# Split exponentials without own waits, a chunk amid the value products, and rows of reciprocal norms by store and broadcast load

## The reference, cut to what matters

```
xn = rmsnorm(x, g_mix)                       # x: (4, 4096, 1024)
u  = xn @ w_in                               # 5120 columns: conv (3x512), q, k, v (512 each), gates (2x1024)
y_a = (b * causal_conv3(c * v_a)) @ w_a_out
s   = q k^T / 8 - slope_h * (qpos - kpos), causal       # 4 heads, two maps of 64 each, values of 128
o   = (softmax(s_1) - lam * softmax(s_2)) v
y_b = (rmsnorm(o) * 0.8) @ w_b_out
x   = x + (sigmoid(g_a) * y_a + sigmoid(g_b) * y_b) @ w_o
x   = x + relu(rmsnorm(x) @ w_mlp_in)^2 @ w_mlp_out
out = rmsnorm(x)
```

## Time and profile before

| what | value |
|---|---|
| median of 3 runs | 1164.12 us (1163.68 to 1166.56) |
| the profiled execution, its own time | 1163.79 us |
| its span on the slowest core (core 5) | 1162.2 us (cores 1160.2 to 1162.2) |
| PE busy | 1127.2 us, 97% |
| ACT, DVE, POOL busy | 47%, 40%, 7% |
| granted TensorE clock, mean of the cores | 0.995 to 0.998 |

### The profile page before, as it was taken

One profiled execution on the slowest core, in us unless ns is written; L12 is line 12 of the kernel. 1 busy time (PEld: TensorE's weight loads), 2 busy tenths in 40 slices (PEclk: granted clock), 3 DMA queues, 4 the chain that ended last, 5 costly groups with the idle time before them and its releaser, 6 DMA issues.

```text
span 1162.2 us, 20430 instructions; the slowest of 8 cores (1160.2 to 1162.2 us)
## 1 busy us (share of the span) xinstructions
PE 1127.2 (97%) x7162; PEld 563.0 (48%) x7162; DVE 466.9 (40%) x1051; ACT 550.3 (47%) x760; POOL 84.3 (7%) x136
## 2 busy tenths in 40 slices
PE   7999999999999999999999999999999999999997
PEld 3444555455455555555544444444444444444444
DVE  2476666644654632433435544222221322223212
ACT  2585786676666888878523223321231033003301
POOL 5212001001001001001100001000000000000000
PEclk8999999999999999999999999999999999999999
DMA  9877522332067059375296686911210140012001
GB/s 140 166 144 138 144 90 51 110 56 46 5 132 147 19 99 179 65 191 105 38 253 168 207 165 172 158 43 55 70 57 1 55 111 17 19 55 73 2 37 55
DMA packets 67491, 111.46 MB, mean 96 GB/s; under 512 B 37216, under 2 KB 40288, under 8 KB 66368
## 3 DMA queue, kind: packets, MB, share of 16 engines
q0 software_dynamic: 15056, 40.22, 22.5%
q1 hardware_dynamic: 52192, 69.68, 20.0%
q10 hardware_dynamic: 144, 0.26, 0.1%
HBM read 114.40 MB, written 29.36 MB: 124 GB/s over the span
## 4 chain that ended last, share of the span: by engine, by line
PE 92%; ACT 3%; DVE 2%; issue 2%; DMA 1%; POOL 0%; DVEq 0%; ACTq 0%; POOLq 0%
PE ps_all L441 92%; ACT big L715 2%; DMA big<-wv 1%; DVE big L780 0%; DVE big L594 0%; DVE big L604 0%; POOL big L484 0%; ACT big L852 0%; DVE big L772 0%; DVE big L863 0%; DVE big L574 0%; ACT big L592 0%; POOL big L446 0%; DVEq L152 0%; DVE big L571 0%
## 5 line engine op out<-in xcount | busy, mean ns | idle before, releaser
L441 PE MATMUL ps_all<-big 128*128 128x512 bf16 (+7 forms) x7162 | 1127.2, 323 | 28.9 <-ACT big L715 8.2
L441 PEld LDWEIGHTS ps_all<-big 128*128 128x128 bf16 (+2 forms) x7162 | 563.0, 98 | 592.9 <-issue 100.7
L715 ACT ACTIVATE big<-ps_all,big 128x1024 bf16<-128x1024 f32 (+3 forms) x384 | 338.3, 926 | 111.4 <-PE ps_all L441 104.4
L982 ACT ACTIVATE big<-ps_all 128x512 bf16<-128x512 f32 x128 | 76.5, 598 | 137.6 <-PE ps_all L441 137.4
L983 DVE TENSOR_TENSOR big<-big 128x512 bf16<-128x512 bf16 x128 | 54.5, 426 | 156.5 <-ACT big L982 156.0
L999 ACT ACTIVATE big<-big 128x1024 bf16<-128x1024 f32 x15 | 15.9, 1057 | 187.9 <-DVE big L994 187.9
L863 DVE SCALAR_TENSOR_TENSOR big<-big,ps_all 128x512 f32<-128x512 f32 x64 | 43.7, 687 | 106.3 <-PE ps_all L441 106.3
L994 DVE SCALAR_TENSOR_TENSOR big<-ps_all,big 128x512 f32<-128x512 f32 x30 | 22.5, 752 | 143.5 <-PE ps_all L441 143.5
L852 ACT ACTIVATE big<-ps_all,big 128x512 f32<-128x512 f32 x64 | 43.6, 686 | 67.7 <-PE ps_all L441 66.6
L898 ACT ACTIVATE big<-big 128x1024 bf16<-128x1024 f32 x16 | 16.9, 1057 | 47.0 <-DVE big L893 47.0
L724 DVE TENSOR_TENSOR big<-big 128x256 bf16<-128x256 bf16 x64 | 18.5, 289 | 46.7 <-ACT big L715 46.6
(11 more groups left out here) (90 smaller groups left out, 296.8 us busy)
## 6 DMA issues: line engine op xcount, KB each, us to landing
big<-xs SPq DMA_DIRECT2D x36, 512.0 KB, 6.8
big<-w POOLq DMA_DIRECT2D x32, 512.0 KB, 8.1
xm_sp<-big SPq DMA_DIRECT2D x16, 512.0 KB, 3.8
big<-xm_sp SPq DMA_DIRECT2D x16, 512.0 KB, 5.8
big<-xT POOLq DMA_DIRECT2D x31, 256.0 KB, 7.6
out<-big SPq DMA_DIRECT2D x15, 512.0 KB, 2.7
xn_sp<-big SPq DMA_DIRECT2D x4, 1024.0 KB, 6.6
big<-wg POOLq DMA_DIRECT2D x8, 512.0 KB, 5.9
```

Source lines behind the costliest of these rows:

```text
L441: S.op("pe", lambda e: e.matmul(out, lhsT, rhs, start=start, stop=stop, skip_group_check=skip), reads, writes)
L715: act(lambda e, a=a, b=b, c=c, s=s, PT=PT, scale=scale: e.activation(PT.ap[:, :, a:b], Sb[s][:, :, a:b], AF.Exp, bias=ccol(C_BTAB + c), sc ...
L982: act(lambda e: e.activation(r.ap, ps, AF.Relu), key, [r])
```

## The change

It has six parts. (1) `op` takes `part`, so the two exponentials of head 0 into one `PT`, and the three copies of the epilogue into `o_raw`, don't wait for each other. (2) `row` takes the place of `bcast` for blocks 1 to 3: a DMA on SP writes rs1 (128x4) to 512 words in HBM, and a second loads them to all 128 partitions of `R_b`. It stands as the last step of `stats`; the three `bcast` chunks leave `W`. (3) The DVE product that makes `ksc` is a step of its own (`scaled`), behind the one that makes rs1. (4) The statistics of block 1 are spread over 7 chunks, from the first pair on, and no longer over 4 from the fourth. (5) In the first pair of a head `pv(n, 0)` stands ahead of the chunk. `until` takes banks 0, 1, 2, 3, 7, starting so that, by the count of the chunks, the last has bank 7. (6) One copy of the halo goes from ACT to DVE.

```diff
+    def op(self, eng, fn, reads=(), writes=(), part=False):
+        return self._add(eng, fn, reads, writes, False, (), part)
...
         def last():
             rstd(rs1[blk], ss1[blk], 4)
-            if blk in ksc:
-                dve(lambda e: e.tensor_scalar_mul(ksc[blk].ap, rs1[blk].ap, 0.125), [rs1[blk]], [ksc[blk]])
+
+        def scaled():
+            dve(lambda e: e.tensor_scalar_mul(ksc[blk].ap, rs1[blk].ap, 0.125), [rs1[blk]], [ksc[blk]])
...
-        return [sq(0), sq(1), sq(2), sq(3), last]
+        return [sq(0), sq(1), sq(2), sq(3), last, scaled if blk in ksc else lambda: row(blk)]
...
+    def row(blk):
+        settle("norm%d" % (blk % 2))
+        S.dma("sp", lambda e: e.dma_start(out=rs_sp[blk].rearrange("(t p) -> p t", p=128), in_=rs1[blk].ap, allow_slow_non_contiguous=True),
+              [rs1[blk]], ["rssp%d" % blk])
+        ld(R_b[blk % 2].ap, rs_sp[blk:blk + 1].partition_broadcast(128), [R_b[blk % 2]], ["rssp%d" % blk])
...
-            act(lambda e: e.copy(hh.ap[:, lo:hi, :], v[:, :, 0, :]), ck, [hh])
+            dve(lambda e: e.tensor_copy(hh.ap[:, lo:hi, :], v[:, :, 0, :]), ck, [hh])
...
+            S.parts.discard(PT)
             for a, b, c in parts:
                 act(lambda e, a=a, b=b, c=c, s=s, PT=PT, scale=scale: e.activation(
                     PT.ap[:, :, a:b], Sb[s][:, :, a:b], AF.Exp, bias=ccol(C_BTAB + c), scale=scale),
-                    Sk[s] + [cst] + ([ksc[blk]] if blk in ksc else []), [PT])
+                    Sk[s] + [cst] + ([ksc[blk]] if blk in ksc else []), [PT], True)
...
-    W += [(0, f) for f in normed(0)] + spread(ks(5)[1:], [])
-    W += spread(vs(5), [halo_stat] + stats(1, 2) + wc_load(0))
+    W += [(0, f) for f in normed(0)]
+    W += spread(ks(5)[1:] + vs(5), stats(1, 2) + [halo_stat] + wc_load(0))
     W += spread(vs(1), xT_steps(2, 2))
-    W += [(1, bcast(1))]
...
-    def until(name, banks=range(8)):
+    def until(name, banks=range(8), turn=False):
         keep, oring[0] = oring[0], Ring(list(banks))
+        if turn:
+            oring[0].i = -sum(w for w, f in W[pos[0]:marks[name]]) % len(banks)
...
-                until(pairs[n + 1]["g"], (7, 0, 1, 2, 3))
+                until(pairs[n + 1]["g"], (0, 1, 2, 3, 7), True)
...
+        lead = p["first"] and n > 0
+        if lead:
+            pv(n, 0)
         if not p["last"]:
             work(2200 - (400 if diag else 0))
-        pv(n, 0)
+        if not lead:
+            pv(n, 0)
         pv(n, 1)
```

More of the change, by code:

```diff
@@ L103, in _add @@
         return ev
-    def op(self, eng, fn, reads=(), writes=()):
-        return self._add(eng, fn, reads, writes, False)
+    def op(self, eng, fn, reads=(), writes=(), part=False):
+        return self._add(eng, fn, reads, writes, False, (), part)
     def dma(self, eng, fn, reads=(), writes=(), extra=(), part=False):
@@ L263, in build_program @@
     xm_sp = dscr("xm_sp", [2048, D], F32)
+    rs_sp = dscr("rs_sp", [4, 512], F32)
     xb_sp = dscr("xb_sp", [2048, D], BF16)
@@ L431, in flush_masks, with act, dve @@
             late_masks.pop(0)()
[L434 to L438, removed]
+    def act(fn, reads, writes, part=False):
+        S.op("act", fn, reads, writes, part)
+    def dve(fn, reads, writes, part=False):
+        S.op("dve", fn, reads, writes, part)
     def mm(out, lhsT, rhs, start, stop, reads, writes, skip=False):
@@ L752, in out @@
             dve(lambda e: e.tensor_copy(o[:, m, 0:3, 0:129], bank(4 + m)[:, 0:390].rearrange(
-                "p (t e) -> p t e", t=3)[:, :, 0:129]), [pk(4 + m)], [o_raw])
+                "p (t e) -> p t e", t=3)[:, :, 0:129]), [pk(4 + m)], [o_raw], True)
+        S.parts.discard(o_raw)
         out(0)
         dve(lambda e: e.tensor_copy(o[:, :, 3, 0:129], bank(6)[:, 0:260].rearrange(
-            "p (m e) -> p m e", m=2)[:, :, 0:129]), [pk(6)], [o_raw])
+            "p (m e) -> p m e", m=2)[:, :, 0:129]), [pk(6)], [o_raw], True)
         out(1)
@@ L1195, in build_program @@
     W += [(0, f) for f in normed(1)]
-    W += spread(vs(2), []) + [(1, bcast(2))] + spread(ks(2)[:2], [])
+    W += spread(vs(2) + ks(2)[:2], [])
     c0 = [(1, f) for f in conv(0)]
@@ L1203, in build_program @@
     W += spread(conv(1)[:11], xT_steps(3, 1))
-    W += [(1, bcast(3))] + [(1, f) for f in conv(1)[11:]]
+    W += [(1, f) for f in conv(1)[11:]]
     W += spread(ks(3) + vs(3) + qs(3), xT_steps(7, 0) + stats(7, None))
```

## The result

The changed kernel takes 1183.91 us (median of 4 runs, 1182.22 to 1185.53) against 1164.05 us before: a ratio of 1.0166, 95% interval 1.0143 to 1.0189. It is some 20 us slower, where 11 us faster was forecast. Some runs have one half of the chip at a lower clock and are some per cent longer; the times and ratios here leave them out. The profiled execution took 1182.22 us, with a span of 1180.7 us on core 3.

What follows compares the result with a forecast made beforehand. PE was taken as the bound, busy 1127.2 of 1162.2 us, other engines mattering only where PE waits. Terms of 14.1 us less 3 given back left 11, so 1153 us from 1163.8; range 1147.5 to 1160.5.

Steps and rivals of the forecast that it cites:

- the two DMAs: Store and load on SP replacing `bcast`: some 7.5 us end to end, under some 20 us of cover, costed at 0.
- The rows come late: Rival: DVE stands at the first product reading `R_b`; decides from 31 us on, 1164 us or more; two slower rivals together 0.06.
- Halved exponentials: Head 0: up to 0.36 us off each of seven PE waits for exponentials; 2.2 us taken, 0.5 if ACT waits elsewhere.
- `ksc`: DVE's `ksc` product as a later step no longer waits for POOL, removing two PE waits: 2.4 us, half as low end.
- `pv(n, 0)` ahead: At heads' starts, value products between two chunks on bank 7 remove eight PE waits: 3.0 us, ends 0 and 4.1.
- Slower by the moved `pv`: Rival: 15 heads' starts each lose 1.0 us more, using up the gain: 1165 us or more; two slower rivals together 0.06.
- Own waits of the epilogue's copies: DVE's second copy at head ends starts 0.17 us late; PE needs copies later: taken as 0, perhaps up to 1 us.
- Banks: `until`: 0.85 us gained before the third group, about 0.9 us lost before the second; together 0, ends -1 and 0.9.
- Statistics, halo, copies: Block 1's statistics earlier 1.2 us (ends -0.5 and 2.4), halo's copy on DVE 0.3 us, epilogue's copies 0.
- The 3 us to be given back again: From the twelfth pair on chunks sit earlier: six new PE waits of about 0.5 us estimated, 3 us lost.
- The first term: Three `bcast` chunks leave PE and full chunks move into their slots: 5.0 us gained, ends 3.3 and 6.2.
- DVE waiting for a DMA ahead of a key's evacuation: Listed among the signs in the later profile that would show the forecast wrong; no size given.

Runs made afterwards that it cites:

- e4: Changed kernel with the three `bcast` back and the three single-word stores still issued but never loaded or read; 1164.83 us, ratio 1.0006.
- e9: Changed kernel with the three `bcast` back instead of the rows, and the `ksc` product back in the step that makes rs1; 1153.64 us.
- e5: Changed kernel with the three `bcast` back instead of the rows, and `pv(n, 0)` back behind the chunk; 1152.76 us.
- e11: Changed kernel with the three `bcast` back instead of the rows, and the first `until`'s banks counted with the halo's one; 1151.01 us.
- e10: Changed kernel storing rows in 16-byte pieces, POOL ordering them where `bcast` stood, the first `until`'s banks counted with the halo's; 1146.98 us.
- e2: Kernel before with only the rows by store and load in place of three `bcast`; 1210.4 us.
- e8: Changed kernel with `bcast` back and unread single-word stores, each word in 512 bytes of its own; 1154.15 us, one run.
- e3: Changed kernel with rows stored as 128 pieces of 16 bytes and `R_b` read with a 16-byte step; 1154.48 us, ratio 0.9913.
- e7: Changed kernel storing rows in 16-byte pieces, POOL ordering them at the end of `row`, the first `until`'s banks counted with the halo's; 1155.8 us.

## Why the prediction was wrong

**The step that failed** is that of the two DMAs, "That cover of some 20 us is why I cost it at 0". The cover was about right: the readers came 27 us (96.68 - 69.56) and 39 us after the issue, 4.3 and 16.2 us of it as waits, so 23 us each. What it had to cover was estimated at 7.5 us from rows that are no bound for it: `on_sp`'s small pieces and a load of 512 KB say nothing of 512 single words into one 2 KB. It was 26.9 us (15.89 + 11.00) and 39.2 us (31.61 + 7.57). The rival "The rows come late" named the place and the price of such a wait, but was held to be four times away; block 2's row went past its 31 us.

**What no case had** is that a slow store costs others: 14.2 us with no reader at all. Neither the sum nor a rival has a term for it. That all engines stop at once behind it is shown; by what is open. Of the third step's 11.9 us the unread store of `e4` accounts for 5.0. In after the waits of 7.9 us and the half clock behind them make nearly all of it, with no wait for a row; why the stand is longer than in `e4` stays open.

**The terms beside the rows** added up to 14.1 - 5.0 = 9.1 us, less 3 given back, 6. They gave some 14.
- Halved exponentials: 2.2, measured 7.0. The 0.18 us were right, the number of places was not. I counted only PE's waits over 0.15 us, seven of them, from the earlier trace rows. But in head 0 of the later groups nearly every pair with an own wait lasts longer by it, with waits of PE mostly too short for that list. What could be counted before is an upper end: 32 of head 0's 40 pairs have two own waits, and 64 of 0.18 us make 11.5 us; 7.0 is six tenths of that.
- `ksc`: 2.4, measured 3.0. In `e9` DVE waits for POOL 2.6 us again, as in the earlier trace rows.
- `pv(n, 0)` ahead: 3.0, measured 2.1, within its ends. In `e5` PE's short waits for L771 at heads' starts are back, 1.7 us in five. The rival *Slower by the moved `pv`* is refuted by it.
- Own waits of the epilogue's copies: held at 0, not tried alone. In the kernel before, DVE's second copy starts 0.73 us after the first, in after 0.47 us, as these lines of the two timelines show (see also the earlier trace rows; it is so in 12 and 14 of the 16 heads):

```profile
375.81 0.56 DVE L752 COPY big<-ps_all 128x387 f32<-128x387 f32 x1
376.54 0.43 DVE L755 COPY big<-ps_all 128x258 f32<-128x258 f32 x1 [0.17 <-PE ps_all L441]
```

```profile
64.75 0.56 DVE L761 COPY big<-ps_all 128x387 f32<-128x387 f32 x1
65.22 0.42 DVE L765 COPY big<-ps_all 128x258 f32<-128x258 f32 x1
```

Here an own wait costs DVE 0.26 us. The Trainium skill, in VectorE: DVE Perf Modes, section The DRAIN you can't avoid, says that the semaphore costs nothing extra; for these copies the trace does not agree. What it is worth to the kernel's time no run shows.

- Banks: the wait ahead of the second group came as counted, and none stands at the third. But its price was wrong: `e11` removes the 0.95 us and gains nothing.
- Statistics, halo, copies: 14.0 - 7.0 - 3.0 - 2.1 = 1.9 us are left for them together, against 1.5 in the sum. With four differences in it, each good to a microsecond or so, that cannot be told from 0; none was tried singly.
- The 3 us to be given back again did not show. They were an estimate without a row, and the runs don't need them.

**The first term** can be read from `e10` against `e11`, which differ in the rows alone: 4.0 us for three `bcast`, with a copy on POOL that is in time. I had 5.0, with ends of 3.3 and 6.2. So the gain by the rows was real, and the two DMAs as the change had them cost some nine times as much.

The changed kernel's profile showed the rest as announced: 8 records of 128x128 fp32 products instead of 32, no wait of DVE for POOL at the `ksc` product, and, as the sign that it went wrong, "DVE waiting for a DMA ahead of a key's evacuation".

## What to carry to other kernels

A DMA of many single words into a small stretch of memory is not priced by its bytes, nor by other small transfers in the trace: leave pieces as long as the source allows and put them in order on an idle engine, at a place where they have long landed, so that nothing stands behind the wait. When a step goes to a DMA, ask not only who waits for it but also what it does to everyone else; a store that nobody reads showed that in one run. And where two engines take turns in a loop, a saving per turn counts by turns, not by the waits long enough to be listed.

## What the hardware showed that I had not expected

- 512 words of 4 bytes into 2 KB of HBM took 11.5 to 35.0 us on the profiled cores (`e4`, after, `e2`); 1.8 to 20.6 us in 512 bytes each (`e8`); 2.3 to 12.9 us as 128 pieces of 16 bytes (`e3`, `e7`, `e10`). The longest of each is the second, right behind the spill, which `e10` moves ahead of it.
- With or shortly behind such a store all engines can stop at once, for 3.5 us in `e4` and 4.7 in after, with no instruction of the core named as what they wait for.
- The granted clock falls behind a stand: after the 15.24 us of PE's wait it is 0.70 from 150 to 155 us, after 4.73 us it is 0.50 from 255 to 260.
- An fp32 operand of DVE read with a step of 16 bytes costs 0.37 to 0.39 us more for 128x512; the same order made by POOL as a copy takes 1.1 us.
